# Merging the branches inside the experts' stage: tiles 2 to 8 one per turn, with a ring of five rows until then

## The reference

```python
wts = softmax(stack(lses, 0), 0)                 # three groups of the dilated branch
od = sum(wts[..., None] * stack(outs, 0), 0)
merged = gt[:, :, 0] * br_gla + gt[:, :, 1] * (od @ w_br_dil) + gt[:, :, 2] * (om @ w_br_mem)
h = x + merged @ w_out                           # gt = sigmoid(gates), (T, 3, 1024)
n2 = rms_norm(h, ln2_g)
# PEER, for each token and each of 8 heads: 16 of 16384 experts
s = einsum('thcd,hckd->thck', (n2 @ peer_wq).reshape(T, 8, 2, 128), peer_keys)
# top 16 of each half, top 16 of their 256 sums -> eidx, gw
act = gelu(einsum('td,thkd->thk', n2, u_tab[eidx])) * gw
y = h + einsum('thk,thkd->td', act, v_tab[eidx])
```

## Time and profile before

| | us |
|---|---|
| median of 3 runs (4655.75 to 4660.61) | 4658.24 |
| the profiled execution, its own time | 4666.81 |
| its span, first to last instruction | 4665.2 |
| merge, first instruction to the experts' first | 1798.17 to 1945.54 |
| experts, first gather issued | 1990.96 |
| experts, PE begins the first pick | 2001.61 |

### The profile page before, as it was taken

The page is one execution under the profiler, slowest core; times in us unless marked ns, Lnnn a source line. Parts: engine busy times, 40 slices in busy tenths (PEclk is TensorE's granted clock), DMA queues, the critical chain, the costliest instruction groups (busy, mean ns, idle before and its releaser), DMA issues.

```text
span 4665.2 us, 55410 instructions
## 1 busy us (share of the span) xinstructions
PE 4163.4 (89%) x18639; PEld 2493.8 (53%) x18639; DVE 2469.0 (53%) x5405; ACT 1744.2 (37%) x4663; POOL 1529.0 (33%) x1390
## 2 busy tenths in 40 slices
PE   7999999997687988899898898898898988988987
PEld 6888888886555764444444444444443443443331
DVE  2111111113843754377667667666676666676665
ACT  2111111113722653244444444444444444444443
POOL 0000000001624531044444444444444444444543
PEclk9999999998888999999999999999999999999999
DMA  8899899794696764599999999999999999999998
GB/s 283 280 321 318 296 317 310 262 300 167 201 348 242 216 180 172 203 387 427 427 427 422 426 421 417 423 423 419 424 417 423 424 415 421 423 424 416 417 417 369
DMA packets 319029, 1635.93 MB, mean 351 GB/s; under 512 B 44721, under 2 KB 87953, under 8 KB 176914
## 3 DMA queue, kind: packets, MB, share of 16 engines
q0 software_dynamic: 162640, 1160.06, 59.8%
q1 hardware_dynamic: 120506, 251.00, 16.0%
q10 hardware_dynamic: 35648, 222.04, 14.5%
HBM read 1547.06 MB, written 311.74 MB: 398 GB/s over the span
## 4 chain that ended last, share of the span: by engine, by line
DMA 32%; PE 17%; ACT 5%; issue 4%; DVE 1%; POOL 0%; DVEq 0%; POOLq 0%; ACTq 0%; PEldq 0%
DMA ex_rows<-scratch_uv,ex_E 32%; PE ex_ps_y L2891 13%; PE ex_ps_q L2839 2%; ACT ex_diag L2590 1%; ACT L2578 1%; ACT ex_w L2582 1%; ACT L2573 1%; ACT ex_gel L2578 1%; PE ex_ps_t L2801 1%; POOL ex_rows L2521 0%; PE ex_ps_y L2885 0%; ACT ex_ex L2573 0%; DVE ex_dots L2735 0%; DVE ex_rows L2735 0%; PE ex_ps_s L2873 0%
## 5 line engine op out<-in xcount | busy, mean ns | idle before, releaser
L2891 PE MATMUL ex_ps_y<-ex_rows,ex_diag 128*128 128x512 f32 (+1 forms) x4224 | 2020.0, 613 | 281.4 <-ACT ex_diag L2590 259.8
L2735 DVE CUSTOM_DVE_ANT_0 ex_rows<-ex_rows,ex_n2u 128x1024 f32<-128x1024 f32 x1056 | 1295.3, 1227 | 869.0 <-DMA ex_rows<-scratch_uv,ex_E 858.9
L2521 POOL DMA_INDIRECT ex_rows<-scratch_uv,ex_E x1056 | 1206.0, 1142 | 1530.1 <-PE ex_ps_y L2891 1389.3
L2891 PEld LDWEIGHTS ex_ps_y<-ex_rows,ex_diag 128*128 128x128 f32 (+1 forms) x4224 | 743.8, 189 | 1405.0 <-ACT ex_diag L2590 720.0
L412 PE MATMUL pj_ps<-pj_w_hi,pj_nT 128*128 128x470 f32 x3072 | 913.7, 377 | 10.6 <-DVE pj_w_lo L248 9.5
L2578 ACT ACTIVATE ex_gel<-ex_dots 128x1 f32<-128x1 f32 x1056 | 214.2, 203 | 1388.1 <-DVE ex_dots L2735 1387.3
L412 PEld LDWEIGHTS pj_ps<-pj_w_hi,pj_nT 128*128 128x128 f32 x3072 | 580.2, 189 | 93.0 <-issue 15.0
L412 PE MATMUL pj_ps<-pj_w_lo,pj_nT 128*128 128x470 f32 x1536 | 578.1, 376 | 0.0
L276 DVE COPY pj_zo<-pj_ps 128x470 f32<-128x470 f32 x96 | 61.4, 646 | 703.8 <-PE pj_ps L412 469.0
L2590 ACT ACTIVATE ex_diag<-ex_ident,ex_w 128x128 f32<-128x128 f32 x1024 | 411.1, 401 | 33.4
L276 ACT COPY pj_zo<-pj_ps 128x470 f32<-128x470 f32 x96 | 51.8, 553 | 808.9 <-PE pj_ps L412 382.4
(11 more groups left out here) (378 smaller groups left out, 3619.6 us busy)
## 6 DMA issues: line engine op xcount, KB each, us to landing
pj_w<-in_w_in POOLq DMA_DIRECT2D x24, 1880.0 KB, 18.1
scratch_z<-pj_zo SPq DMA_DIRECT2D x192, 235.0 KB, 13.3
scratch_uv<-in_peer_u ACTq DMA_DIRECT2D x8, 4096.0 KB, 25.7
scratch_uv<-in_peer_v ACTq DMA_DIRECT2D x8, 4096.0 KB, 43.7
scratch_uv<-in_peer_u ACTq DMA_DIRECT2D x4, 8192.0 KB, 42.9
scratch_uv<-in_peer_v ACTq DMA_DIRECT2D x4, 8192.0 KB, 73.9
out_dk_s<-in_cache_dil_k ACTq DMA_DIRECT2D x8, 4088.0 KB, 44.5
out_dv_s<-in_cache_dil_v ACTq DMA_DIRECT2D x8, 4088.0 KB, 56.1
```

Of the source, the lines that this page charges most:

```text
L2521: pool.indirect_dma_start(out=rows[:, p % SLOTS, :], out_offset=None, in_=d["uv"], in_offset=bass.IndirectOffsetOnAxis(ap=E[:, turn % 4, k ...
L2735: nc.vector.tensor_tensor_reduce(out=row, in0=row, in1=n2u[:, tile % 2], scale=1.0, scalar=0.0, op0=ALU.mult, op1=ALU.add, accum_out=dots[ ...
L2891: last = nc.tensor.matmul(y[0:n, 512 * c:512 * c + 512], diag[:, p % DIAGS, 0:n], rows[:, p % SLOTS, D + 512 * c:D + 512 * c + 512], start ...
```

## The change

The `merge` stage is gone. `attend` ends with more: it loads all tiles' `lse` and tile 0's groups (at `n == ASK + 6`), works out the mixing weights of all eight tiles at once and mixes tile 0 (`first_mixed`), and it stores the last branch tile one step earlier. `experts` begins with the merges of tile 0 and, around the first queries, of tile 1. Tiles 2 to 8 are merged in turns 0 to 6, one per turn, between the picks (`in_turn`). Their buffers (`gate_gla`, `turned_two`) are the places of rows 5 to 7 of the ring, so the ring has 5 rows for picks 0 to 119 and 8 from pick 120 on; POOL takes the first of the three new places only when the last merged tile is stored. `w_q` no longer lies in SBUF whole: heads come one at a time into two buffers for turns 1 to 7, 9 and 10 (`STREAM`), and heads 3 to 7 then go where `wb` and `od` were. The mixing multiply moves from POOL to DVE. Semaphores of a stage are cleared ahead of the next block (`clear_used`), inside the barrier that ends the stage, and the second barrier is gone. The last five pieces of the diff are SP's, POOL's, ACT's, DVE's and PE's.

```diff
-    def give_back():
-        nc.clear_and_free_semaphores(taken)
-        nc.all_engine_barrier()
-    ctx.callback(give_back)
+    ctx.callback(lambda: d["used_up"].extend(taken))
...
-    SLOTS = 8
+    IN_TURNS = NT - 1
+    FEW, SLOTS = 5, 8
+    ALL_FROM = (IN_TURNS * K + K // 2) // FEW * FEW
+    STREAM = (1, 2, 3, 4, 5, 6, 7, 9, 10)
+    PRODUCT_AT = (5, 6, 8, 9, 10, 11, 13, 14)
...
+        def slot_of(p):
+            return p % FEW if p < ALL_FROM else (p - ALL_FROM + FEW) % SLOTS
+        def held_before(p):
+            if p < ALL_FROM:
+                return p - FEW if p >= FEW else None
+            return p - SLOTS if p >= ALL_FROM + SLOTS - FEW else None
+        def in_turn(turn):
+            return turn + 2 if turn < IN_TURNS else None
...
+            for turn in range(IN_TURNS):
+                tile = in_turn(turn)
+                if tile + 1 < TILES:
+                    load_groups(tile + 1)
...
+                if turn + 4 < len(STREAM):
+                    load_head(turn + 4)
+                for b in range(3):
+                    if tile + 1 < TILES:
+                        if b == 0:
+                            sp.wait_ge(first, tile + 1)
+                        else:
+                            sp.wait_ge(gated, NPRD * tile + 2 * b)
+                        load_gate(tile + 1, b)
+                sp.wait_ge(added, NPRD * (tile + 1))
+                sp.dma_start(d["h"][tokens(tile), :], a_gla[0:width(tile)]).then_inc(m_stored, 16)
+                if tile + 1 < TILES:
+                    sp.wait_ge(m_stored, 16 * (tile - 1))
+                    load_gla(tile + 1)
...
-                    if p >= SLOTS:
-                        pool.wait_ge(v_done, p - SLOTS + 1)
+                    if held_before(p) is not None:
+                        pool.wait_ge(v_done, held_before(p) + 1)
+                    elif p >= FEW:
+                        pool.wait_ge(m_stored, 16 * IN_TURNS)
...
+                    if in_turn(turn) is not None:
+                        if k == 4:
+                            turned_branches(in_turn(turn))
+                        if k == 6:
+                            gate_values(in_turn(turn))
...
+                    if k == 1 and turn and in_turn(turn - 1) is not None:
+                        gated_part(in_turn(turn - 1), 3)
+                    if tile is not None:
+                        if k == 8:
+                            first_gated(tile)
+                        if k in (9, 12, 14):
+                            gated_part(tile, (9, 12, 14).index(k))
+                        if k in (10, 11, 13) and tile + 1 < TILES:
+                            mixed(tile + 1, (10, 11, 13).index(k))
...
+                    if tile is not None:
+                        if k == 2:
+                            turn_branches(tile)
+                        if k in PRODUCT_AT:
+                            q, half = divmod(PRODUCT_AT.index(k), 2)
+                            product(tile, q, (half,))
```

More of the change, by code:

```diff
@@ L2757, in normed_rows @@
                                                op0=ALU.mult, op1=ALU.mult).then_inc(n2_done, 1)
+            first_gated(0)
+            for q in range(NPRD):
+                gated_part(0, q)
+            for part in range(3):
+                mixed(1, part)
+            first_gated(1)
             added_rows(0)
@@ L2762, in _ @@
             normed_rows(0)
-            for turn in range(2):
-                for part in range(K):
-                    route(turn, part)
+            gated_part(1, 0)
+            for part in range(K):
+                route(0, part)
+            gated_part(1, 1)
+            gated_part(1, 2)
+            for part in range(K):
+                route(1, part)
+            gated_part(1, 3)
+            for part in range(3):
+                mixed(2, part)
             for turn in range(TURNS):
+                tile = in_turn(turn)
                 for k in range(K):
@@ L2804, in out_product, with turn_branches @@
                     last.then_inc(h_prod, 1)
-            turn_merged(0)
-            for part in range(2 * KD):
-                out_product(0, part)
-            pe.wait_ge(consts_in, 48)
-            pe.wait_ge(keys_in, 16 * 2 * PH)
-            for g in range(2):
+            def turn_branches(tile):
+                n = width(tile)
+                pe.wait_ge(b_in, 32 * (tile + 1))
+                pe.wait_ge(od_done, tile + 1)
+                if tile:
+                    pe.wait_ge(gated, 2 if tile == 1 else NPRD * tile)
+                for k in range(KB):
+                    at = k * P + (D if k >= 4 else 0)
+                    last = nc.tensor.transpose(ps_y[:, 1, k * P:k * P + n], od[0:n, at:at + P], ident[0:n, 0:n])
+                last.then_inc(a_t, 1)
@@ L2897, in sum_row @@
                     pe.sem_inc(y_sum, 1)
-            for turn in range(3):
-                if opens(turn):
-                    turn_rows(turn)
-                queries(turn)
-                scores(turn)
+            pe.wait_ge(d["wb_in"], 32)
+            turn_branches(0)
+            product(0, 0)
+            pe.wait_ge(keys_in, 16 * 2 * PH)
+            turn_keys(0)
+            turn_keys(1)
+            product(0, 1)
+            product(0, 2)
+            product(0, 3)
+            turn_merged(0)
+            for part in range(2 * KD):
+                out_product(0, part)
+            turn_branches(1)
+            product(1, 0)
+            pe.wait_ge(consts_in, 48)
+            turn_rows(0)
+            queries(0)
+            scores(0)
+            product(1, 1)
+            queries(1)
+            product(1, 2)
+            scores(1)
+            queries(2)
+            product(1, 3)
+            scores(2)
             for turn in range(TURNS):
```

559 lines of the change are left out of this document (279 added, 280 removed).

## The result

The changed kernel takes 4687.52 us (median of 4 runs, 4683.07 to 4691.66) against 4657.82 (4 runs) of the kernel before: 1.0059 times as long, 95% interval 1.0044 to 1.0075. It is slower by 30 us; 4644 us were forecast. Its profiled execution took 4687.93 us, its median's time, while that of before, 4666.81 us, was 9.0 us over the median of these four runs (8.6 over the 4658.24 of the three before the prediction), so the two profiles differ by 21 us only.

A forecast was written before the change was run, and what follows sets the result against it. Merge was taken as bound by PE, the picks by DMA with PE close behind. Terms -113.3 - 2.4 + 66.9 + 25 + 15 - 4 - 1.2 = -14.0 us gave 4644 us, range 4618 to 4692.

The forecast's parts named there:

- the exchange: Seven tiles of PE-bound merge, 105 us, move into DMA-bound picks that leave PE about 6 us a turn free.
- The prologue's steps: Experts' start to PE's first pick: keys at +14.5, first scores +67.7, first pick +95.0 us; saves 113.3 us.
- 344.2 + 25: Turns 0 to 6: PE's work by pitch 344.2 us, plus 25 us of gaps from late rows and ACT, bounds 0 to 80.
- the 5.8 us of a gather alone: Landing time assumed for the ring of five in turns 0 to 6, leaving 5 us of slack, 2 in the light stretch.
- After turn 6: From pick 112 on: held heads +15, handover -4, tile 1 not through DRAM -1.2 us; POOL's wait covered.
- The sign named for this stretch: From pick 112 to the end, about 15 us more than before would show the forecast right.
- +15 held heads: After turn 6: heads 3 to 7, 5.2 MB, load while DMA is full, 12.3 to 15.1 us, taken as +15.
- -4 two rows ready: At the handover after turn 6, two rows are ready before PE instead of none, saving 4 us.
- Smooth: Turns 0 to 6: the ring hides all gaps and PE runs at its pitch; -39 us, 4619; chance 18%.
- ACT pays the drain: Sigmoid table switches in turns 0 to 6 also pay about 1.38 us of drain each; -3 us, 4655; chance 7%.
- SP's chain is late: SP's in-order store, then GLA load, exceeds 21.5 us in turns 0 to 6; +25 in all, 4683; chance 20%.
- The ring of five starves: Turns 0 to 6: gathers keep 14.9 us, a pick takes 3.9 us; sum +54, 4712; chance 10%.

The follow-up runs named there:

- the last of these kernels: Changed kernel, ring at a multiple of 512 bytes, with 16-column merge loads for tiles 3 to 8 and no sigmoid for tiles 2 to 8: turns 0 to 6 346.7 us.
- With the ring aligned: Changed kernel with the 64 bytes of `iota` allocated behind the ring, which then begins at a multiple of 512 bytes: 4652.38 us, ratio 0.9985 to the kernel before.
- the kernel with the heads reordered as well: Changed kernel, ring at a multiple of 512 bytes, a semaphore per held head, heads 4 to 7 loaded behind tile 2's rows and x: 4650.55 us, ratio 0.9970.

## Why the prediction was wrong

**Right: the exchange.** The prologue's steps came out nearly one by one. After the stage's start at 1783.17 PE has the keys at +14.5 (forecast +14.5), DVE the first scores at +66.7 (+67.7), PE the first pick at +93.2 (+95.0). The changed kernel's timelines of PE, DVE, POOL and PE again at these places:

```profile
1797.66 1.54 PE L2866 MATMUL ex_ps_t<-mg_ident,ex_n2u 128*128 128x128 f32 x6 [5.95 <-DMA ex_yo<-in_peer_keys]
...
1849.85 0.49 DVE L2653 MAX8 ex_top<-ex_sc 128x8 f32<-128x128 f32 x2 [9.34 <-ACT ex_sc L2511]
...
1858.22 1.08 POOL L2449 DMA_INDIRECT ex_rows<-scratch_uv,ex_E  x1 [107.95 <-DVE ex_E L2712]
...
1876.34 4.63 PE L2954 MATMUL ex_ps_y<-ex_rows,ex_diag 128*128 128x512 f32 x5 [6.77 <-ACT ex_diag L2532]
```

They answer to the earlier trace rows. Turns 0 to 6 were to take 344.2 + 25 = 369.2 and took 369.9. That this comes within 1 us is luck: the 25 held a margin for what wasn't seen, and kernels with the same turns differ by up to 7 us. PE's share there is 0.95, the DMA share 0.99 (a little above the 0.9 to 0.97 named). The gathers of turns 0 to 6 in the changed kernel, issue to landing:

```profile
DMA to landing us min/median/max: 5.6/9.1/13.8
```

Inside the 7 to 11 us forecast. The 25 us of gaps had the right size and the right causes, late rows and ACT, as the last of these kernels shows. Their inner working was off. One number was the 5.8 us of a gather alone, where 8.3 is what five in flight take (9.1 beside the merge): it left 5 us of slack on paper, of which 2.5 to 3.3 were not there. And the gaps are not in turns 1 to 4 alone: from turn 0 to turn 6 PE stood 0.0, 3.2, 1.9, 2.8, 4.7, 3.3 and 3.0 us, where turns 5 and 6 were to have under 2 each.

**Wrong: the picks after turn 6 at their old rate.** "After turn 6" costs the held heads, POOL's wait, the handover and tile 1, and takes for granted that the picks from 120 on cost what they cost before, at the 427 GB/s of the earlier trace rows. This is the step that failed: a term of 0, put there without a reason, where 30.3 us were measured. With the ring aligned, turn 10 to the end took 2262.6 us (a span of 4651.7, from 2389.1 on) against 2263.1 before and 2293.4 in the changed kernel, so all of it is the ring's place. I costed what the buffers' new places do to waits and order, not what their addresses do. The sum is off by 35.1 us: 30.3 here, 13.7 in turns 7 to 9, 0.7 in turns 0 to 6, less 2.3 for the prologue and 7.3 ahead of it. With the ring aligned the kernel is 0.15% faster than before, on the forecast's side, whose -0.30% it doesn't reach; the kernel with the heads reordered as well does (0.9970). The sign named for this stretch, about 15 us more from pick 112 to the end, came out as 53.8 (23.5 and 30.3). That the measured 4687.5 us still lies within 4618 to 4692 is luck: the upper end was there for a late chain on SP in turns 0 to 6, and the time was lost behind them.

The Trainium skill (DMA: Bandwidth & Descriptors, How a descriptor splits into AXI transactions) says that a transaction must start at a multiple of 256 bytes, so that a descriptor which doesn't start there pays for more beats (of 32 bytes). It speaks of reads; here the written side is off. An estimate from that section of the Trainium skill: a row 64 bytes past needs 258 beats instead of 256, 128 past 260, +0.8% and +1.6%. The queue rows above show 1.1 to 1.4% fewer bytes at 64 past and 1.3% at 128: the boundary agrees with the Trainium skill, the growth with the distance does not show.

**Mis-sized: what comes after turn 6.** The term "+15 held heads" was right as bytes (15.4). What I left out is that several such loads in a row hold SP's queue: the four long issues, three heads and the store behind them, took 66 us in the changed kernel and 81 with each head waited for. In the first PE stood 24 us for the last head, in the second 24 us for the rows of tile 2 behind them: +6. That it is the 1 KB pieces which fill the queue is argued, not tested; a single issue of 7 MB took 0.38 us in the kernel before (1945.54), so the size of one load isn't it. "-4 two rows ready" is not seen on its own.

**The rivals.** *Smooth* didn't come: PE idled 18.8 us. *ACT pays the drain* didn't come either. ACT in the changed kernel at pick 6 of turn 1:

```profile
1945.19 1.28 ACT L2466 ACT_TABLE_LOAD   x1
1946.48 2.76 ACT L2466 ACTIVATE ex_gate_gla<-ex_gate_gla 128x3072 f32<-128x3072 f32 x1
1949.26 1.28 ACT L2520 ACT_TABLE_LOAD   x1
1950.56 0.20 ACT L2520 ACTIVATE ex_gel<-ex_dots 128x1 f32<-128x1 f32 x1
```

The loads follow and are followed within 0.02 us, as in the earlier trace rows; a drain of 1.38 us shows at none of them. *SP's chain is late*: in turns 0 to 6 DVE waited for the GLA tile 1.5 us in all, so not there; but its core, a queue in order with a late load behind long issues, is what happened in turn 8. *The ring of five starves*: not at 14.9 us a landing, but alone it costs 22.9 us, which the merge's slower pitch for the most part hides (346.7 us with the loads and the sigmoid gone).

Not settled: why a row 64 and one 128 bytes past cost the same, and why part of the slow packets take 312 and part 319 ns. What the ring of five costs beside the merge was not measured apart, since there is no room for eight rows.

## What to carry to other kernels

When buffers move, compare the start of each gather's or load's destination modulo 256 bytes before and after, and read GB/s beside the DMA share: the share stays at 1 when packets get slower. Before putting several long loads on a queue, ask what is issued behind them. Giving each its own semaphore does nothing while the queue itself stands. A ring's depth is to be checked with the landing at that depth, not with that of a lone transfer.

## What the runs showed of the hardware

- A 128 x 8192 B gather into rows that begin 64 or 128 bytes past a multiple of 256 moves 415 to 416 GB/s, into rows at a multiple 421 to 422: 34 to 37 us for 1056 gathers. Packets of 4096 bytes had a median of 159 ns in all of these kernels.
- Loads of 1 MB in 1 KB pieces beside a full gather queue: the first issue took 0.43 us, the second 2.11, the third and fourth 18.58 and 20.62, while the loads landed 21 us apart.
- A 1 MB gather of 128 rows landed after 5.8 us as the first one, 8.3 with a ring of five (median) and 14.9 with a ring of eight.
- A DMA share of 0.99 to 1.01 came with 387, 391, 405, 416 and 422 GB/s.
